# Two-layer block, one core: the second layer's latents from un-normalised x, squares folded by VectorE, value unit and key rotations earlier

## What is computed

```
x1  = x + mixed @ w_out                      # end of block one ("out1")
y   = rmsnorm(x1, final_norm_gain)           # residual stream of block two
h   = rmsnorm(y, attn_norm_2)                # what block two's projections read
z   = h @ w_in_2  ->  c_q 768, c_kv 256, k_r 32, q, k, v 3 x 512, two gates 2 x 1024
MLA:  q = rmsnorm(c_q) @ w_uq ; k_nope, v = rmsnorm(c_kv) @ w_ukv ; rotary on parts of q and k
MoBA: attention of q, k, v, with rotary on 16 of 64 columns
```

## Time and profile before

| what | value |
|---|---|
| median of the runs | 792.1 us (790.5, 792.1, 795.67) |
| profiled execution, its own time | 794.2 us |
| its span in the trace | 792.4 us |
| busy: PE, PEld | 691.7 us (87%), 578.0 us (73%) |
| busy: DVE, ACT, POOL | 354.9 us (45%), 325.6 us (41%), 386.7 us (49%) |
| DMA over the span | 181.73 MB, mean 229 GB/s |
| mean granted TensorE clock | 0.96 |

### The profile page before, as it was taken

How to read it: one execution, slowest core, us unless ns; L and a number is a source line. 1 busy time by engine, 2 the same in 40 slices (tenths; PEclk the granted TensorE clock), 3 DMA queues, 4 the chain that set the end, 5 groups by cost and what they waited for, 6 DMA issues and landing times.

```text
span 792.4 us, 13896 instructions
## 1 busy us (share of the span) xinstructions
PE 691.7 (87%) x5658; PEld 578.0 (73%) x5658; DVE 354.9 (45%) x657; ACT 325.6 (41%) x589; POOL 386.7 (49%) x284
## 2 busy tenths in 40 slices
PE   3799999999999989699988999989799997777764
PEld 3789989889989988699777899989654544333421
DVE  1788964489997131610692554561520111001002
ACT  5434566875464334445434766432312121111112
POOL 2656865588879978098597656695000000000000
PEclk9978999999999999799988999999999999999998
DMA  8613543433344445045343433489979999999992
GB/s 331 248 54 107 167 148 112 158 109 124 142 161 158 162 160 172 41 160 191 129 160 107 160 108 117 150 356 419 380 274 423 421 421 420 422 421 423 421 422 117
DMA packets 26131, 181.73 MB, mean 229 GB/s; under 512 B 3025, under 2 KB 3281, under 8 KB 4561
## 3 DMA queue, kind: packets, MB, share of 16 engines
q1 hardware_dynamic: 26064, 180.81, 59.9%
HBM read 179.75 MB, written 1.05 MB: 228 GB/s over the span
## 4 chain that ended last, share of the span: by engine, by line
PE 60%; DMA 15%; DVE 13%; ACT 5%; issue 4%; SPq 1%; POOL 0%; ACTq 0%; DVEq 0%
PE D L447 39%; PE L L832 4%; DMA ring<-w_expert_dram 4%; DMA hT<-w_expert_dram 4%; DMA wu<-w_expert_dram 4%; DMA big<-w_expert_dram 3%; PE L L812 3%; DVE big_r L1328 2%; PE QB L862 2%; PE UB L488 1%; DVE big_r L1333 1%; PE L L575 1%; DVE big L1469 1%; SPq L386 1%; DVE big L1309 1%
## 5 line engine op out<-in xcount | busy, mean ns | idle before, releaser
L1292 POOL TENSOR_TENSOR ring_r<-ring,ring_r 128x512 fp32r<-128x512 f32 x280 | 386.5, 1410 | 161.0 <-ACT ring_r L950 160.4
L447 PE MATMUL D<-scr_r,ring_r 128*128 128x256 f32 x1248 | 239.7, 289 | 1.7 <-ACT big L1179 0.9
L950 ACT ACTIVATE ring_r<-ring 128x1024 fp32r<-128x1024 f32 x140 | 147.3, 1057 | 151.4 <-PE D L447 133.1
L447 PEld LDWEIGHTS D<-scr_r,ring_r 128*128 128x128 f32 x1248 | 199.1, 193 | 4.6 <-issue 2.1
L447 PE MATMUL D<-hT_r,ring_r 128*128 128x256 f32 x624 | 177.3, 284 | 0.0
L447 PE MATMUL D<-big_r,ring_r 128*128 128x256 f32 x1158 | 146.8, 288 | 9.8 <-DVE big L1600 5.2
L447 PEld LDWEIGHTS D<-big_r,ring_r 128*128 128x128 f32 x1158 | 143.8, 196 | 11.4 <-DVE big L1600 5.6
L447 PEld LDWEIGHTS D<-hT_r,ring_r 128*128 128x128 f32 x624 | 120.5, 193 | 1.2 <-issue 1.0
L1309 DVE SCALAR_TENSOR_TENSOR th<-th,L 64x256 f32<-64x256 f32 x32 | 13.4, 418 | 179.1 <-ACT th L1223 178.5
L1223 ACT ACTIVATE th<-L 64x256 f32<-64x256 f32 x16 | 6.0, 378 | 85.7 <-PE L L832 85.7
L812 PEld LDWEIGHTS L<-cst,big 128*128 128x128 f32 x256 | 29.8, 191 | 12.2 <-issue 10.7
(11 more groups left out here) (302 smaller groups left out, 934.5 us busy)
## 6 DMA issues: line engine op xcount, KB each, us to landing
ring<-w_dense_dram SPq DMA_DIRECT2D x70, 1024.0 KB, 4.9
big<-w_expert_dram SPq DMA_DIRECT2D x40, 1024.0 KB, 25.8
ring<-w_expert_dram SPq DMA_DIRECT2D x30, 1024.0 KB, 26.2
wu<-w_expert_dram SPq DMA_DIRECT2D x6, 1024.0 KB, 25.1
attn<-w_expert_dram SPq DMA_DIRECT2D x5, 1024.0 KB, 21.3
scr<-w_expert_dram SPq DMA_DIRECT2D x5, 1024.0 KB, 27.0
hT<-w_expert_dram SPq DMA_DIRECT2D x5, 1024.0 KB, 27.3
xT<-w_expert_dram SPq DMA_DIRECT2D x5, 1024.0 KB, 27.6
```

What stands on the lines that cost most here:

```text
L447: last = mm(out_, r32(w[i][ws]), r32(x[j][xs_]), start=start and m == 0, stop=stop and m == 2)
L950: A_(r32(hi_unit(j)), dense_unit(j), ACT.Copy).then_inc(hi_ready, 1)
L1292: last = g.tensor_tensor(r32(w), w, r32(h).bitcast(F32), ALU.subtract)
```

## The change

It does five things. (1) The chunks of `cq` and `ckv2` read `x1` = x1 times both gains, without the per-token factors; ScalarE rounds it to `x1_hi` and VectorE makes `x1_lo` in four pieces, as `out1` gives them. The latents' own norms use `raw_ms`, in which the missing factor is put back beside the eps. `h` itself is still made and is read from `qb` on. (2) ScalarE squares piece by piece and VectorE adds the squares of four pieces (`fold`), so that TensorE has 2 matmuls with ones for each sum where it had 8; these stand after the second and the third chunk of `cq`. (3) `swap` 2 and 3 go into `vb`; `rotate` 2 and 3 go ahead of the rotary key. (4) The value unit `ukvv` goes ahead of the key unit `ukvk`, with the first pair of scores between them. (5) VectorE writes the rotary key once (32 x 256) and ScalarE copies it into the eight heads; the sums of squares of the latents move to after `qb` and into `kb`.

```diff
-    ("vb", [4, 4], "act"), ("uq", [2, 4, 6, 8], "dve"), ("ukvk", [1, 1], "act"),
-    ("ukvv", [1, 1], "act"), ("gates", [2, 4, 6, 8, 10, 12, 14, 16], "act"),
+    ("vb", [4, 4], "act"), ("uq", [2, 4, 6, 8], "dve"), ("ukvv", [1, 1], "act"),
+    ("ukvk", [1, 1], "act"), ("gates", [2, 4, 6, 8, 10, 12, 14, 16], "act"),
...
-            sumsq(N_FIN1)
-
+            x1 = (x1_hi, x1_lo)
+
+            def sum_folded(n, dst, src):
+
+                pe.wait_ge(folded, n - N_FIN1 + 1)
+                for c in range(2):
+                    last = mm(dst[:, 0:T], ones, src[:, c, :], start=(c == 0), stop=(c == 1))
+                last.then_inc(ssq, 1)
+
+            chunk("cq", 0, x1, split="x1")
+            chunk("cq", 1, x1)
             pe.wait_ge(o_ready, 8)
-            for c in range(DC):
-                pe.wait_ge(sq, SQ0[N_ATT2] + c // 2 + 1)
-                last = mm(QB[:, 0:T], ones, m_hi[:, c, :], start=(c == 0), stop=(c == DC - 1))
-            last.then_inc(ssq, 1)
-
-
-            for c in range(6):
-                chunk("cq", c, h2, split="att2" if c == 0 else None)
+            pe.wait_ge(rooted, N_FIN1)
+            sum_folded(N_FIN1, UB, scr)
+            chunk("cq", 2, x1)
+            sum_folded(N_ATT2, QB, hT)
+            for c in range(3, 6):
+                chunk("cq", c, x1)
             for c in range(2):
-                chunk("ckv2", c, h2)
+                chunk("ckv2", c, x1)
             for c in range(4):
-                chunk("qb", c, h2)
+                chunk("qb", c, h2, split="att2" if c == 0 else None)
+            sumsq(N_CQ, src=cq_sq)
             for c in range(4):
                 chunk("kb", c, h2)
+                if c == 0:
+                    sumsq(N_CKV2, src=ck_sq)
...
-            sumsq(N_CQ, src=cq_sq)
-            sumsq(N_CKV2, src=ck_sq)
...
                                np.s_[:, (k % 2) * 512:(k % 2 + 1) * 512], k == 0, k == DC - 1)
                 if k % 2:
                     last.then_inc(unit_done, 1)
+                if k >= 5 and k % 2:
+                    swap(k // 2)
             pe.wait_ge(lo_of["wkr"], 1)
             for k in range(DC):
                 last = mm3(QB[0:2 * ROPE, 0:T], (wkr_hi, wkr), h2, np.s_[:, k, :], np.s_[:, k, :], k == 0, k == DC - 1)
             last.then_inc(kr_mm, 1)
-            swap(2)
-            swap(3)
             for h in range(H2):
                 chunk("uq", h, (cq_hi, cqT), kc=QC, split="cq" if h == 0 else None)
             pe.wait_ge(lo_of["ck"], 1)
+            w = unit(UNIT0["ukvv"])
+            for tt in range(NT):
+                bank = open_bank("ukvv", tt)
+                for k in range(KC):
+                    last = mm3(bank[:, 0:512], (ck_hi, ckT), w, np.s_[:, k, tt * P:(tt + 1) * P],
+                               np.s_[:, k * 512:(k + 1) * 512], k == 0, k == KC - 1)
+            last.then_inc(unit_done, 1)
+
+
+            def moba_scores(m):
+                score_pair(H1 + 2 * m, lambda j, tt: qb[HD2 * j:HD2 * (j + 1), m, tt * P:(tt + 1) * P],
+                           lambda j, n: kb[HD2 * j:HD2 * (j + 1), m, 0:n])
+
+            pe.wait_ge(rotated, 4)
+            kept(pe, "vb", 1)
+            moba_scores(0)
             w = unit(UNIT0["ukvk"])
             for m in range(4):
                 bank = open_bank("ukvk", m // 2) if m % 2 == 0 else DB[(FILL0["ukvk"] + m // 2) % 2]
...
-                bank = open_bank("ukvv", tt)
-                for k in range(KC):
-                    last = mm3(bank[:, 0:512], (ck_hi, ckT), w, np.s_[:, k, tt * P:(tt + 1) * P],
-                               np.s_[:, k * 512:(k + 1) * 512], k == 0, k == KC - 1)
-            last.then_inc(unit_done, 1)
...
+            for i in range(4):
+                advance(UNITS_AT[FILL0["out1"] + i] + HI_UNITS - (i == 3))
+                kept(act, "out1", i)
+                for c in (2 * i, 2 * i + 1):
+                    last = A_(r32(x1_hi[:, c, :]), xT[:, c, :], ACT.Copy, scale=both_gains[:, c:c + 1])
+                last.then_inc(hi_of["x1"], 1)
+                A_(scr[:, 2 * i:2 * i + 2, :], xT[:, 2 * i:2 * i + 2, :], ACT.Square).then_inc(sq, 1)
+                for c in (2 * i, 2 * i + 1):
+                    last = A_(hT[:, c, :], xT[:, c, :], ACT.Square, scale=V("final_norm_gain", c))
+                last.then_inc(sq, 1)
             advance(UNITS_AT[FILL0["out1"] + 3] + HI_UNITS)
-            squares(N_FIN1, x1_src(act, "out1"))
-
-            act.wait_ge(unit_done, UNITS_AT[FILL0["out1"] + 3])
-            for c in range(DC):
-                last = A_(m_hi[:, c, :], xT[:, c, :], ACT.Square, scale=V("final_norm_gain", c))
-                if c % 2:
-                    last.then_inc(sq, 1)
+
+            def keep(stage, i, dst, n=2):
+                bank = filled(act, stage, i)
+                A_(dst, bank[:, :].rearrange("p (a b) -> p a b", a=n), ACT.Copy).then_inc(rel["act"], 1)
+
+            act.wait_ge(unit_done, UNITS_AT[FILL0["aproj"] + 3])
+            keep("cq", 0, cqT[:, 0:2, :])
             rootmean(N_FIN1)
+            advance(UNIT0["cq"] + 3 + HI_UNITS)
             act.wait_ge(ms2_ready, 1)
             act.wait_ge(rinvd, N_ATT2)
             A_(root[:], ss2, ACT.Sqrt, bias=sp[:, 9, 0:1], scale=1.0 / D).then_inc(rooted, 1)
+            keep("cq", 1, cqT[:, 2:4, :])
...
-                keep("kb", i, kb[:, 2 * i:2 * i + 2, :])
-            rootmean(N_CQ)
-            rootmean(N_CKV2)
+                keep("qb", i, qb[:, 2 * i:2 * i + 2, :])
+
+            def root_raw(n):
+
+                act.wait_ge(ms2_ready, n - N_CQ + 2)
+                act.wait_ge(rinvd, n)
+                A_(root[:], raw_ms, ACT.Sqrt).then_inc(rooted, 1)
+
+            root_raw(N_CQ)
+            keep("kb", 0, kb[:, 0:2, :])
             round_pieces("cq", cqT, cq_hi, lambda i: act.wait_ge(normed, NM0[N_CQ] + 2 * i + 2), 3)
+            root_raw(N_CKV2)
             round_pieces("ck", ckT, ck_hi, lambda i: act.wait_ge(normed, NM0[N_CKV2] + 2), 1)
+            keep("kb", 1, kb[:, 2:4, :])
             for i in range(2):
                 bank = filled(act, "vb", i)
                 A_(vb[:, i, :], bank[:, :], ACT.Copy).then_inc(rel["act"], 1)
+            act.wait_ge(kr_ready, 1)
+            A_(kh[64:96, :, :], rinv[64:96, :].unsqueeze(1).to_broadcast([32, H2, T]), ACT.Copy).then_inc(kr_ready, 1)
...
-            out_end("out1")
-            kept(dve, "out1", 3)
+            def fold(src, i, ready):
+
+                dve.wait_ge(sq, ready)
+                ins = v.tensor_tensor(src[:, 0:2, :], src[:, 0:2, :], src[:, 2 * i:2 * i + 2, :], ALU.add)
+                ins.then_inc(folded, 1) if i == 3 else step(ins)
+
+            for i in range(4):
+                out_end("out1", i)
+                kept(dve, "out1", i)
+                dve.wait_ge(hi_of["x1"], i + 1)
+                for c in (2 * i, 2 * i + 1):
+                    last = stt(r32(x1_lo[:, c, :]), xT[:, c, :], both_gains[:, c:c + 1],
+                               r32(x1_hi[:, c, :]).bitcast(F32), ALU.mult, ALU.subtract)
+                last.then_inc(lo_of["x1"], 1)
+                if i:
+                    fold(scr, i, SQ0[N_FIN1] + 2 * i + 1)
+                    fold(hT, i, SQ0[N_FIN1] + 2 * i + 2)
 
             dve.wait_ge(rooted, N_FIN1 + 1)
             dve.wait_ge(normed, NM0[N_FIN1])
             v.reciprocal(rinv[:], root[:]).then_inc(rinvd, 1)
+            v.tensor_scalar(eps_s2, UB[:, 0:T], 1.0 / D, EPS, ALU.mult, ALU.add)
             dve.wait_ge(rinvd, N_FIN1 + 1)
             dve.wait_ge(ssq, N_ATT2 + 1)
             step(v.tensor_tensor(ss2, QB[:, 0:T], rinv[:], ALU.mult))
             v.tensor_tensor(ss2, ss2, rinv[:], ALU.mult).then_inc(ms2_ready, 1)
             dve.wait_ge(ms2_ready, 1)
+            step(v.tensor_scalar(raw_ms, ss2, 1.0 / D, EPS, ALU.mult, ALU.add))
 
...
             rest_of("att2", hT, scr)
+            step(stt(eps_s2, raw_ms, EPS, eps_s2))
...
+            def raw_mean(n):
+                dve.wait_ge(ssq, n + 1)
+                stt(raw_ms, UB[:, 0:T], 1.0 / NORMS[n][1], eps_s2, ALU.mult, ALU.add).then_inc(ms2_ready, 1)
```

67 lines of the change are left out of this document (31 added, 36 removed).

## The result

The changed kernel takes 783.98 us (median of 4 runs, 781.9 to 786.2); the kernel before, timed beside it, 793.23 (4 runs, 790.5 to 795.67). The ratio is 0.9892, 95% interval 0.9871 to 0.9913. That is faster and clear of the noise, by 9.2 us (1.1%), where 20.6 were forecast; 771.5 was predicted, and 783.98 lies above the range of 765 to 780. The profiled execution took 784.96 us, its span is 783.2.

The account below looks back on a forecast made before the run. TensorE was taken to set the pace until the DMA-bound last third. Gain 15.7 at the join, 13.3 by `uq`, 21.6 by the gates, less 1 for the clock: 20.6, so 771.5 us; forecast 768 to 775, range 765 to 780.

Parts of the forecast that it names:

- The bound: Whole kernel: TensorE sets the pace ahead of the last third, where the stream of expert weights does.
- the rival that it does not arrive: Experts: the weight stream ends when it always did, so the time stays at 789 to 793 us; chance 0.04.
- the one that it is slower: From the join to the gates: GpSimd is locked out by VectorE, up to 800 us; chance 0.03.
- The join: From `out1` through eight latent units: the chain ahead of `cq` goes, the units end at 340.0 us, gain 15.7.
- GpSimd beside VectorE ... Costed at nothing: In `out1`: GpSimd falls 3.6 us behind over three banks, within its lead of 5.1; 1 us kept for the range.
- `h` ready with some 4 us to spare: At the first `qb` chunk, 340 us: the last rest is done near 336, so TensorE finds `h` ready.
- The wait before `vb`: Second key bank: ScalarE empties it behind both latents' root and rounding; TensorE waits some 2.5 us, bounds 0 to 4.
- The preparation: From `uq` to the gates: the 3.7 us stall goes, GpSimd sets the end of `uq`; gates at 415.5 us.
- that is late next: rotary key: In `uq`: ScalarE's rotary key copy lasts until 390.5 us, and only then is `uq` 4 rounded, 391.6.
- The clock: Up to the gates: waits of 1 to 2.5 us may bring the lower clock; 1 us taken off the gain.
- attention, gates and closing projections are unchanged: From the gates to the end: these stages stay as they were, and the DMA-bound stretch keeps its length.
- Rival (a): Preparation: half given back through GpSimd at 3.38 us a unit, the key bank and low clock; 775 to 781, chance 0.16.

Follow-up runs that it names:

- f4: The changed kernel with four edits: folds behind all rests, rotary key copied later, second key bank emptied earlier, norm factors in PSUM; 772.05 us.
- g3: f4 with the first pair of scores moved behind the key unit; 769.01 us.
- e4: The changed kernel with the per-token factors of the norms written to PSUM instead of SBUF; 782.46 us.
- g2: The changed kernel with two edits: folds behind all rests and the norms' factors in PSUM; 776.27 us.
- f1: The kernel before with only the later half of the change (swaps, rotations, rotary key, value unit ahead of key unit); 793.51 us.
- f2: The changed kernel with the later half (swaps, rotations, rotary key, order of value and key unit) undone; 783.18 us.
- h1: The changed kernel with only the first pair of scores moved behind the key unit; 782.30 us.
- e3: The changed kernel with the second key bank emptied by ScalarE ahead of the root of the second latent; 782.46 us.

## Why the prediction failed, step by step

**The bound, right.** TensorE set the pace up to the experts, every microsecond won at the gates arrived at the end but for the clock, and neither the rival that it does not arrive nor the one that it is slower came true. With four further edits that remove waits the forecast is reached: f4 took 772.05, with 124.4 us in A where 125.9 were predicted. With the moved line as well, g3 is 23.7 us faster than the kernel before (792.73 - 769.01).

**The join, direction right, 15.7 mis-sized.** From the first `cq` matmul the eighth unit should have ended 25.4 us later; it ended about 29.1 us later (342.8 - 313.7). The "0.5 us of waiting in it, and no fall of the clock" was 2.83 us and a chunk of 4.32 instead of 2.89. The two sums at 1.8 us were right (2.05).

**The step that failed: "GpSimd beside VectorE ... Costed at nothing".** It asked only whether GpSimd, delayed by VectorE, would still be in time for TensorE. In `out1` it was: GpSimd took 1.26 to 1.53 us a half unit there (2.51 for two, 6.11 for four), and TensorE did not wait for it. The other direction was not priced: VectorE's own operations, delayed by GpSimd. The rows had it, four rests at 4.39 us instead of 2.49, and were read as each losing what the other used; here a product lost 1.0 us and a half unit 0.2. The eight `hT` products were taken at 3.26, the price beside an idle GpSimd, and took 4.16; the two norms that now run beside a full one took 11.42 and 8.35. The rule quoted from the Trainium skill, page "SBUF — State Buffer", section "Who interferes with whom", names both engines as locked out and was applied to one. e4 shows the mechanism. Its price in time is g2's 7.7 us, of the 11.4 by which the forecast missed (20.6 - 9.2).

**"`h` ready with some 4 us to spare": wrong.** The fourth rounded piece was due near 334 to 336 and came at 339.1, and the first `qb` chunk waited 1.1 us for its unit, rounded behind it. Here GpSimd was late too: it was counted at 2.55 us a unit and took 2.21 for the first half, beside VectorE, and 1.45 for the second, up to 343.8, where 2.55 would have ended at 342.7, just before TensorE was free (342.8). In e4 this wait is gone.

**The wait before `vb`: mechanism right, size wrong.** 2.5 us were forecast (0 to 4), 3.9 measured; the surplus is the norm of 8.35 us ahead of ScalarE's rounding (in e4, where the norm takes 2.44, the wait is 1.8). Together 2.3 (first chunk), 1.4 (its clock), 1.1 (`qb`) and 1.4 (here) come to 6.2, against the 6.1 us by which `cq` to `vb` is too long in the table.

**The preparation: half right.** The stall for the turned queries went, and "that is late next: rotary key" was right: the copy ended at 397.9, and GpSimd stood still for 5.0 us behind it. Forecast were 8.3 us of gain between `uq` and gates, 5.9 came. f1 and f2 show that in this kernel nothing of it reaches the end.

**The clock: 1 us counted, at least 4 paid.** 3.1 us in B, and most of the 1.7 in `vb` to `uq`, where the wait of 3.9 left the clock at 0.67 from 376 to 380 us. The 1.6 us of `out1` are not the prediction's error but this execution's. The step "attention, gates and closing projections are unchanged" holds for the instructions, not for the clock at which they run.

Rival (a), half given back in the preparation, came nearest, 775 to 781; it named the key bank's 4 us and the low clock, but gave the cause to GpSimd's rate, and stopped at 781 for want of VectorE's own delay.

## What to carry to other kernels

Where one engine's two-input SBUF operations lie beside GpSimd's, price both engines: here about one VectorE operation went through for each of GpSimd's, so the short ones grew, from 0.4 to 1.4 us, and the long ones by 0.2. Keep one operand of repeated VectorE products in PSUM where a bank is free, and put additions that nobody awaits yet behind the operation that someone does. Read an edit of a few microseconds off the stretch it changes and off the median, and see first whether an untouched stretch of the reference trace is as long as in the other traces; here 1.6 us were not. Try small independent matmuls in a wait of 2 us of TensorE even where the next stage does not start earlier; here that gave 3.0 and 1.7 us (g3, h1), and why is not shown in full.

## What the runs showed of the hardware

The place of one operand decided the contention: eight products of 128 x 256 took 11.42 us with both inputs in SBUF and 3.22 with one in PSUM, both beside a busy GpSimd.

The clock does not follow from a wait alone: after the same wait of 3.0 us in the router it stayed at 1.00 in the kernel after and fell to 0.50 in e4, 3 us apart in time. What a dip costs depends on where it falls: at `out2` in the kernel before (0.81 and 0.77 from 528 to 536 us) and in h1 it lay in a wait for VectorE and cost nothing.

B comes in steps. From the first gates matmul to `out2` it is 92.8 us in six of the fourteen traces (before, e3, f2, g1, g3, h1) and 94.2 or 94.3 in the other eight; from there to the sums ahead of the router 25.6 or 25.7 in the same six but e3, and 26.9 to 27.2 in the other nine. So in g3, where 0.8 us of a wait before the gates went, the loss there and the one at `out2` went together, and in thirteen traces they stand or fall together; e3 has the second without the first. What ties them stays open. The Trainium skill, page "TensorE: Matmul & The Clock Gate", section "What's actually happening", says that the number of slow matmuls at the start of one and the same kernel differs from run to run. It says so of the start; the two router stretches and the starts of `out1` show as much in the middle of a kernel.
